# One more third of a token tile by gathered rows: the first 128 tokens instead of 96, with the routing stage's low parts moved from VectorE to GpSimd

## The reference, cut to what matters

```python
s = jnp.einsum("thpc,pkc->thpk", q, sub_keys)          # scores against 2 x 128 half keys, 8 heads
s1, i1 = lax.top_k(s[:, :, 0], 16); s2, i2 = lax.top_k(s[:, :, 1], 16)
top_s, pos = lax.top_k(cand_s, 16)                     # best 16 of the 16 x 16 sums, for each head
gate = jax.nn.softmax(top_s, axis=-1)
...
u = u_tab[ib]                                          # 128 experts for each token, 1024 numbers each
act = jax.nn.gelu(jnp.einsum("td,ted->te", xb, u), approximate=False)
return jnp.einsum("te,ted->td", act * gb, v_tab[ib])
```

## Time and profile before

| | |
|---|---|
| Median of 3 runs | 2227.98 us (2227.13 to 2233.2) |
| Profiled execution: time, span | 2232.91 us, 2231.2 us |
| Mean granted TensorE clock | 0.974 of full speed |
| PE busy | 2069.1 us (93%) |
| DVE, ACT, POOL busy | 1405.5, 829.9, 445.4 us |
| DMA moved | 396.68 MB in 239664 packets, 114912 of them under 512 B |
| The store of a 64-token block of gates | 4096 KB, 28.1 us from issue to landing |
| A load of a U chunk | 512 KB, 4.0 us |

### The profile page before, as it was taken

How to read it: one execution, slowest core, us unless ns; L and a number is a source line. 1 busy time by engine, 2 the same in 40 slices (tenths; PEclk the granted TensorE clock), 3 DMA queues, 4 the chain that set the end, 5 groups by cost and what they waited for, 6 DMA issues and landing times.

```text
span 2231.2 us, 30598 instructions
## 1 busy us (share of the span) xinstructions
PE 2069.1 (93%) x11732; PEld 1844.5 (83%) x11732; DVE 1405.5 (63%) x2647; ACT 829.9 (37%) x1271; POOL 445.4 (20%) x557
## 2 busy tenths in 40 slices
PE   7889888889988799999999998888999999999999
PEld 7766666666656578889999998888999999999999
DVE  5442442532532564399999687777277777777777
ACT  4333433432432443233333465555333333333332
POOL 3132032032031100001000132221022323232322
PEclk9999999999999799999999999999999999999999
DMA  3210200200200642246554599999789999999996
GB/s 117 71 38 1 80 30 11 75 25 10 76 29 10 213 153 76 78 126 184 174 168 146 170 268 271 278 270 268 261 291 325 325 326 319 325 319 323 321 325 234
DMA packets 239664, 396.68 MB, mean 178 GB/s; under 512 B 114912, under 2 KB 164256, under 8 KB 239520
## 3 DMA queue, kind: packets, MB, share of 16 engines
q1 hardware_dynamic: 209568, 287.66, 40.5%
q0 software_dynamic: 29952, 107.07, 14.3%
HBM read 335.85 MB, written 58.72 MB: 177 GB/s over the span
## 4 chain that ended last, share of the span: by engine, by line
PE 54%; DVE 5%; DMA 5%; ACT 1%; issue 1%; SPq 0%; ACTq 0%; DVEq 0%
PE psE L84 17%; PE psE L86 17%; PE psE L85 17%; DMA raw<-in_peer_u 4%; DVE shared L1706 1%; PE psE L1911 1%; ACT expert_hi L1381 1%; PE psE L1912 1%; DVE expert_lo L1538 1%; PE psE L1869 1%; DVE shared L1613 1%; DVE few_gathered L1695 1%; DMA raw<-in_w_mixers 0%; DVE half_index L1617 0%; DVE w_lo L1748 0%
## 5 line engine op out<-in xcount | busy, mean ns | idle before, releaser
L1381 ACT ACTIVATE expert_hi<-raw 128x1024 fp32r<-128x1024 f32 x288 | 305.0, 1059 | 522.1 <-PE psE L86 446.9
L1538 DVE TENSOR_TENSOR expert_lo<-raw,expert_hi 128x1024 fp32r<-128x1024 f32 x288 | 351.8, 1223 | 214.2 <-ACT expert_hi L1381 211.5
L84 PE MATMUL psE<-w_hi,expert_hi 128*128 128x416 f32 x1024 | 360.9, 352 | 15.5 <-DVE w_lo L1748 15.5
L84 PE MATMUL psE<-x2h,expert_hi 128*128 128x416 f32 x1024 | 368.0, 359 | 5.0 <-DVE expert_lo L1538 5.0
L86 PE MATMUL psE<-x2h,expert_lo 128*128 128x416 f32 x1024 | 361.3, 353 | 0.0
L85 PE MATMUL psE<-x2l,expert_hi 128*128 128x416 f32 x1024 | 360.9, 352 | 0.0
L85 PE MATMUL psE<-w_lo,expert_hi 128*128 128x416 f32 x1024 | 358.8, 350 | 0.0
L86 PE MATMUL psE<-w_hi,expert_lo 128*128 128x416 f32 x1024 | 358.7, 350 | 0.0
L84 PEld LDWEIGHTS psE<-w_hi,expert_hi 128*128 128x128 f32 x1024 | 192.2, 188 | 25.7 <-issue 20.9
L84 PEld LDWEIGHTS psE<-x2h,expert_hi 128*128 128x128 f32 x1024 | 194.6, 190 | 8.2 <-DVE expert_lo L1538 6.7
L85 PEld LDWEIGHTS psE<-x2l,expert_hi 128*128 128x128 f32 x1024 | 194.9, 190 | 2.1
(11 more groups left out here) (290 smaller groups left out, 3544.8 us busy)
## 6 DMA issues: line engine op xcount, KB each, us to landing
raw<-in_peer_u SPq DMA_DIRECT2D x128, 512.0 KB, 4.0
raw<-in_peer_v SPq DMA_DIRECT2D x128, 512.0 KB, 6.5
expert_acts<-gelu SPq DMA_DIRECT2D x128, 208.0 KB, 4.9
shared<-expert_acts SPq DMA_DIRECT2D x128, 208.0 KB, 4.2
shared<-expert_gates SPq DMA_DIRECT2D x128, 176.0 KB, 5.5
expert_gates<-shared SPq DMA_DIRECT2D x5, 4096.0 KB, 28.1
ring<-in_w_xonly SPq DMA_DIRECT2D x24, 512.0 KB, 3.4
ring<-in_w_full SPq DMA_DIRECT2D x16, 512.0 KB, 3.9
```

Of the source, the lines that this page charges most:

```text
L84: nc.tensor.matmul(out, sh, mh, start=first, stop=False)
L1381: nc.scalar.activation(wh[:, s % R, :], raw[:, s % R, :], ACT.Copy).then_inc(S["hi_done"], 1)
L1538: v.tensor_tensor(wl[:, s % R, :], raw[:, s % R, :], wh[:, s % R, :].bitcast(F32), ALU.subtract).then_inc(S["lo_done"], 1)
```

## The change

FEW becomes 128 and MANY 384: the first tile of tokens is wholly gathered, one token to a partition, with no spreading, no groups and no `fold`. The steps are 128 dots and 128 additions (before: 96 and 96). 78 dots stand between the routing steps of tiles 1 to 3, 26 to a tile, over `few_ring`; 46 beside the pairs and 4 behind them, over `u_ring`; the additions all in the V stage. The rows of x stay in PSUM (`rows_x`, two banks), and the dots read them there. In the U stage the low parts of chunks 3 to 78 are written by GpSimd, in the same queue as the gathers; VectorE writes those from 79 on. A tile's turn comes at chunks 34, 55 and 76 (ROUTED_AT) and the pairs begin at chunk 76: 48 pairs. The DRAM tensor of the gates is laid out by blocks, so that a block's store is 32 KB in one piece for each partition; the V stage loads gates for 4 chunks at once, in pieces of 1 KB. The loads at the start of `back` are in another order, and two loads on GpSimd wait for the mixers' high parts.

```diff
-GROUPS = ((0, 64), (64, 32))
-FEW = sum(count for _, count in GROUPS)
-FIRST_OPS = 48
+FEW = P
+TILE_DOTS = 26
+ROUTE_DOTS = (NT - 1) * TILE_DOTS
+FIRST_DOTS = P
 MANY = SEQ - FEW
-ROUTE_CHUNKS = 16
-PAIRS_A = NT * ROUTE_CHUNKS
+ROUTED_AT = (13, 34, 55, 76)
+PAIRS_A = ROUTED_AT[-1]
-STORED = MANY - BLOCK
+STORED = (BLOCKS - 1) * BLOCK
+GATE_CHUNKS = 4
+        rows_x = ps[:, ROW_BANK:ROW_BANK + 2, :].rearrange("p b d -> p (b d)")
...
             def store_rows(b):
-                t0, t1 = max(b * BLOCK - SHIFT * GATE_TOKENS, 0), (b + 1) * BLOCK - SHIFT * GATE_TOKENS
-                sp.dma_start(gates_dram[:, :, t0:t1].rearrange("j i t -> i j t"),
-                             rows[b % 2][:, :, BLOCK - (t1 - t0):]).then_inc(rows_stored[b % 2], 16)
+                sp.wait_ge(S["gates_moved"], 2 * PER_BLOCK * (b + 1))
+                sp.dma_start(gates_dram[:, b, :, :], rows[b % 2]).then_inc(rows_stored[b % 2], 16)
...
-                sp.dma_start(gates_in[:, r, :], gates_dram[j]).then_inc(w_loaded[r], 16)
+                if j % GATE_CHUNKS == 0:
+                    slot = j // GATE_CHUNKS % 2
+                    sp.dma_start(gates_in[:, slot, :, :, :], gates_dram[:, :, j:j + GATE_CHUNKS, :]).then_inc(
+                        gates_loaded[slot], 16)
...
         def _(pool):
+            def low(s):
+                pool.wait_ge(S["lo_done"], s)
+                pool.wait_ge(S["hi_done"], s + 1)
+                nc.gpsimd.tensor_tensor(wl[:, s % R, :], raw[:, s % R, :], wh[:, s % R, :].bitcast(F32),
+                                        ALU.subtract).then_inc(S["lo_done"], 1)
+            pool.wait_ge(S["mixed_hi"], DC - 2)
...
+            for j in range(3, ROUTED_AT[0]):
+                low(U + j)
             pool.wait_ge(S["few_picked"], 2)
-            for g, (t0, count) in enumerate(GROUPS):
-                for f in range(P // count):
-                    for out_, in_ in ((which[g], picked_expert), (few_gate[g], picked_gate)):
-                        pool.dma_start(out_[f * count:(f + 1) * count, :],
-                                       in_[t0:t0 + count, f * count:(f + 1) * count]).then_inc(few_spread, 16)
+            for n in range(R):
+                gather(n)
+            sent = R
+            for j in range(ROUTED_AT[0], PAIRS_A + 3):
+                low(U + j)
+                while sent < min(R + (j + 1 - ROUTED_AT[0]) * ROUTE_DOTS // (PAIRS_A - ROUTED_AT[0]), ROUTE_DOTS):
+                    gather(sent)
+                    sent += 1
...
             def turn_rows(k):
-                for (t0, count), b in zip(GROUPS, ROW_BANKS):
-                    for f in range(P // count):
-                        last = nc.tensor.matmul(
-                            ps[f * count:(f + 1) * count, b + k // 4, (k % 4) * P:(k % 4 + 1) * P],
-                            normed[:, k % 2, t0:t0 + count], c["ident"][:, :], start=True, stop=True)
+                nc.tensor.matmul(ps[:, ROW_BANK + k // 4, (k % 4) * P:(k % 4 + 1) * P], normed[:, k % 2, 0:FEW],
+                                 c["ident"][:, :], start=True, stop=True).then_inc(S["rows_turned"], 1)
```

More of the change, by code:

```diff
@@ L1191 @@
 BLOCKS = -(-MANY // BLOCK)
-SHIFT = (BLOCKS * BLOCK - MANY) // GATE_TOKENS
-STORED = MANY - BLOCK
+STORED = (BLOCKS - 1) * BLOCK
+GATE_CHUNKS = 4
 STORES = [len(range(b, BLOCKS - 1, 2)) for b in range(2)]
 HALF_ROWS = KEYS * BLOCK
[L1196 to L1199, removed]
+ROW_BANK = 0
+TURN_BANK = 2
+GELU_AT = 1
 MIX, OUT, QUERY, U, V = 0, DC, 2 * DC, 4 * DC, 4 * DC + KEYS
@@ L1295, in back @@
         gathered = [sem(f"few_gathered{r}") for r in range(R)]
-        few_spread = sem("few_spread")
+        gates_loaded = [sem(f"gates_loaded{r}") for r in range(2)]
         mixed_loaded = [sem(f"mixed_loaded{k}") for k in range(DC)]
@@ L1347, in _ @@
                 sp.dma_start(mixer_out[:, k, :], mixed[k]).then_inc(mixed_loaded[k], 16)
-                if k % 4 == 3:
-                    load(k // 4 + 1)
-            load(3)
+            for r in range(1, R):
+                load(r)
             sp.dma_start(keys[:, :, :], ap["keys"]).then_inc(keys_loaded, 16)
@@ L1594, in take_query @@
                 v.tensor_tensor(query[:, q % 2, :], ps[:, 2 + q % 2, :], rstd[:, :], ALU.mult).then_inc(S["query_ready"], 1)
-            ahead = itertools.chain([None] * 3, range(3, N))
-            def low_next():
-                j = next(ahead)
-                if j is not None:
-                    low(U + j)
+            few = itertools.count()
+            gaps = itertools.count()
+            def dots_next():
[3 more added lines that the diff above has]
+                        few_next()
             count = 0
@@ L1749, in low_w @@
                                 ALU.subtract).then_inc(S["w_lo_done"], 1)
-            done = 0
-            for t0, few in GROUPS:
-                v.tensor_copy(fold[:, t0:t0 + few], c["ident"][:, 0:few]).then_inc(S["folded"], 1)
-                for f in range(1, P // few):
-                    done += 1
-                    dve.wait_ge(S["folded"], done)
-                    v.tensor_tensor(fold[:, t0:t0 + few], fold[:, t0:t0 + few],
-                                    c["ident"][:, f * few:(f + 1) * few], ALU.add).then_inc(S["folded"], 1)
-                done += 1
             low(0)
@@ L1762, in _ @@
                 mixed_row(k)
-                if k == 3:
-                    low(1)
+            low(1)
             for m in range(DC):
@@ L1785, in _ @@
                 route(i)
-            low_next()
             take(NT - 1)
+            dve.wait_ge(S["lo_done"], U + PAIRS_A + 3)
             for p in range(PAIRS_B):
                 one_hot(p)
-                if 2 <= p < 2 + FIRST_OPS:
-                    few_first(p - 2)
-                low_next()
-            for j in ahead:
-                low(U + j)
+                if p >= 2:
+                    few_next()
+                low(U + PAIRS_A + 3 + p)
+            trailing = FIRST_DOTS - ROUTE_DOTS - (PAIRS_B - 2)
+            rest = N - PAIRS_A - 3 - PAIRS_B
+            for k in range(rest):
+                for _ in range(k * trailing // rest, (k + 1) * trailing // rest):
+                    few_next()
+                low(U + N - rest + k)
             low(V)
@@ L1805, in _ @@
                     low(V + j + 3)
[L1806 to L1809 removed]
+                if j == GELU_AT + 2:
+                    few_weigh()
+                for _ in range(few_upto(j - 1) if j else FIRST_DOTS, few_upto(j)):
+                    few_next()
                 if j + 1 < N:
@@ L1950, in _ @@
                 activations(j)
-                if j < PAIRS_A + 1 and j % ROUTE_CHUNKS == 0 and j > 0:
-                    turn(j // ROUTE_CHUNKS - 1)
+                if j in ROUTED_AT[1:]:
+                    turn(ROUTED_AT.index(j))
                 if PAIRS_A <= j < PAIRS_A + PAIRS_B:
```

188 lines of the change are left out of this document (83 added, 105 removed).

## The result

The changed kernel takes 2156.75 us (median of 4 runs, 2155.93 to 2159.93) against 2227.89 before: ratio 0.968, 95% interval 0.966 to 0.970. That is 71 us faster where 120 were forecast, and 2 us above the range. The profiled execution took 2157.28 us with a span of 2155.5, 75.6 under its counterpart before.

What follows compares the result with a forecast made beforehand. TensorE, busy nearly throughout the expert stages, was taken as the bound, a matmul's price going by columns. -83.6 - 3.8 - 5.8 - 26 + 12 - 13 = -120 on 2228.0 gave 2108 us, range 2080 to 2155.

Steps and rivals of the forecast that it cites:

- columns, 6144 matmuls: Expert stages: matmuls go from 416 to 384 columns, a step of 175.2 ns, 13.6 ns less each; -83.6 us.
- start of the U stage: Before U: row turning, six matmuls become one, saves 5.3 us, reordered first loads perhaps 0.5; together -5.8 us.
- loss in the routing: Routing beside U: new losses 7 + 6 + 4 = 17 us, some 5 of old idling gone; +12, bounds -5 and +62.
- loss in V: V stage: of 21 us lost, 8 left, 4 for double turns and 4 for transfers; -13 us.
- Rival C: Expert matmuls: the 0.19 us weight load binds, so fewer columns give nothing; 2192 us, chance 0.03.
- it fits in 4.205, barely: V stage: chain from ScalarE's hi to w_lo's end, 3.96 us plus about 0.1, fits a 4.205 us chunk.
- Rival A: Pairs and V: transfers bind, shorter chunks ask more than DMA gives; up to 2160 us, half 2134, chance 0.20.
- large packets are nearer to V's row: Store at the pairs: of a remaining loss between 0 and 46 us, takes 8; with 34 gone, -26 us.
- Exclusion of VectorE's operations and GpSimd's: Routing tiles: VectorE operations with two SBUF inputs wait for GpSimd lows, 0 to 12 us a tile, 6 taken.
- The stall of 7 us for the low of chunk 13: Routing: GpSimd waits for tile 0's experts, issues four gathers, then the low at 1008.5; TensorE wants it at 1001.3.
- rival B: Routing: GpSimd binds, in-order gathers behind dots and lows of 2.6 us; some 50 us, 2146 us, chance 0.18.
- Rival D: Routing: slower than before, VectorE holds up GpSimd's lows, chunk 6.1 us or more; 2284 us at 7 us, chance 0.03.

Runs made afterwards that it cites:

- e1: Changed kernel, V stage writes the low part of the next chunk's activations ahead of the weights' low part and the addition; 2133.1 us, ratio 0.957.
- e12: e10 with each block's store sent in four quarters, one chunk apart; 2091.0 us, ratio 0.939.
- e5: Changed kernel with the old DRAM layout of the gates, in pieces of 256 bytes; 2189.7 us, ratio 0.982.
- e11: Changed kernel without the gathers beside the pairs (48 of 50 over u_ring left out, dots kept, output differs); 2131.2 us, ratio 0.957.
- e13: e12 with V's first loads (activations of the first four chunks and their gates) two chunks earlier; 2081.5 us, ratio 0.934.
- e2: Changed kernel with rank and index of the candidates in PSUM instead of SBUF; 2141.4 us, ratio 0.960.
- e3: Changed kernel with tile 0's exponents and gathers four chunks later (ROUTED_AT 17 for 13); 2153.7 us, ratio 0.967.
- e8: Changed kernel with the diffs of e2 and e3 together; 2146.0 us, ratio 0.962.
- e10: Changed kernel with the edits of e1, e2 and e9 together; 2106.5 us, ratio 0.945.
- e9: e2 with a tile's 26 dots spread over the 16 gaps by the time VectorE has, not evenly; 2137.3 us, ratio 0.958.

## Why the prediction was wrong

Losses are what a stage takes over its chunks at the step's price and its pairs at 0.96 us. Between the starts of the table lie 65 chunks, 51 chunks with pairs and 12 chunks before, and 77, 47 and 4 after (us of the profiled executions):

| term of the sum | forecast | measured |
|---|---|---|
| columns, 6144 matmuls | -83.6 | -95.2 |
| four pairs fewer | -3.8 | -3.8 (taken) |
| start of the U stage | -5.8 | -14.2 |
| loss in the routing | +12 | +33.0 (12.0 to 45.0) |
| loss at the pairs | -26 | -17.3 (39.1 to 21.8) |
| loss at the turn to V | 0 | +11.0 (0.2 to 11.2) |
| loss in V | -13 | +10.7 (20.3 to 31.0) |

The last four are 21.0 + 8.7 + 11.0 + 23.7 = 64 us worse, the first and the third 11.6 + 8.4 = 20 better; 120 + 20 - 64 = 76 is what the two executions differ by. Two starting points were misread: from the first pair's start to the last one's are 51 steps and not 52, so that 39 us were lost there and not 34, and V took 600.1 us by the earlier trace rows, not 601.

*Columns: right, a little small.* A step of 173.3 ns, under both of my lines, so a matmul of 384 columns saves 15.5 ns and not 13.6. Rival C, the weight load as a floor, is out: the load still reads 0.19 us, and the step fell.

*Start of U: right in kind.* The merge, from its first matmul to its last, is 8.4 us shorter (740.6 to 944.0 before, 734.9 to 929.9 after), in place of 5.8. The other 5.7 arise in the first 735 us, where the change only puts two small tables elsewhere in SBUF. With one and the same code there, that point lies between 732.3 and 741.2 in the profiled executions of after and of the twelve experiments, and the 740.6 of before lies within. Between 160 and 180 us the granted clock was 0.83 before and 1.00 after. So nothing here shows that these 5.7 are the change's.

*V: the step "it fits in 4.205, barely" failed*, and it is the dearest. It compared the chain from the start of `hi` to the end of `w_lo` with a chunk, and left out the ends that close the loop: 0.21 us from the chunk's first matmul to `hi`, and 0.15 from `w_lo` to the next matmul. The trace of before had it: a chunk's first matmul started at 1691.27 and `hi` at 1691.53, so that 0.26 + 3.96 + 0.15 = 4.37 was under the 4.53 of a chunk then, and over 4.205. That with TensorE faster the bound would pass to this chain was among my signs of error, but no rival had it, and I priced it at nothing. e1 shows it: same bytes, same work, other order, 26 us less in V. Timeline of TensorE, before:

```profile
1691.27 0.35 PE L84 MATMUL psE<-w_hi,expert_hi 128*128 128x416 f32 x1
```

*Rival A, transfers bind:* out as I meant it, for e1 and e12 move the same bytes faster, at 334 and 326 GB/s. The 324 of before was what was asked for.

*The store: right on SP, wrong on what stays.* The issue of 20.50 us is gone, and e5 brings it back, at 12 us in the pairs. I worked out the rest as volume against rate and took 8. What stayed was one transfer's landing: a gather of 512 KB beside the 4 MB store lands in some 10 us, over two slots, and the low and the one-hots stand behind it in VectorE's queue. e11 takes the gathers away, e12 the burst, and the stage is 244.9 and 244.8 us, 4 over 47 x 5.12, so that 17.6 of the 21.8 were this wait. The step that failed is "large packets are nearer to V's row". I asked what the dots beside the pairs cost VectorE and DMA, not what they wait for.

*The turn to V: not in the sum.* ScalarE's `w_hi(0)` needs gates loaded after the last store and weighed, 11.3 us late; before, the loss there was nothing (54.6 us for 12 chunks of 4.53). e13 and e11 take off 5.4 and 9.8 of it, from its two ends.

*Routing: right in kind, a third in size.* Exclusion of VectorE's operations and GpSimd's was priced at 2 us a tile, 6 in all, and the part of it that e2 takes away cost 17.4 us, since it stretches the gathers too, and what GpSimd loses shows as TensorE's wait. The stall of 7 us for the low of chunk 13 didn't come: GpSimd waited 3.75 us for tile 0's experts, and TensorE 1.36 us for the low. Another stood there that I didn't name: ScalarE's exponents of tile 0, in the queue ahead of `hi` and gelu, hold TensorE for 8 us, five chunks earlier. Nor may that be added as it stands, for e3 and e8 remove it and the stage gets no shorter. That GpSimd and VectorE wait for each other in turn, so that time won at one tile is lost at the next, is my reading of the waits that grew. Of rival B's 50 us two thirds came: the loss in the stage grew by 33, though GpSimd is busy for only 238 of 280 us in the window and waits for others in the rest. Rival D is out with lows of 2574 ns.

*Open.* 22 us are still lost in the routing of e13 (342.4 against 77 x 4.16 = 320.3). In e10, with the same routing, the wait behind the exponents (7.8), those for lows (5.5) and the first pair's for its one-hot matrices (3.9, as in the kernel before) account for 17. What the lower clock beside that first wait adds is argued from the window of 0.74 and wasn't tried by itself. The exponents were moved only together with tile 0's gathers (e3, e8), and not with the order of dots of e9.

## What to carry to other kernels

When an edit makes the bounding engine faster, take each loop of waits that closes once per tile and add all of it: the releasing instruction, each start behind it, the semaphore, the weight load. One that had under 0.2 us of room (4.37 in 4.53) becomes the bound, and here the cure was to swap two instructions. Moving work to an idle engine must be priced by what stands behind it in each queue, with the landing time of its transfers during the largest burst beside it; and a queue's stall that seems to be one event may be a lockstep that comes back elsewhere.

## What the hardware did that I had not expected

- An indirect gather's issue on GpSimd took 2.82 to 3.06 us beside VectorE's compares with two inputs in SBUF, for 0.94 alone; the mean of the stage's gathers fell from 1124 to 969 ns when one of these inputs lay in PSUM. VectorE's side paid as well: 2890 ns on the mean for 2280.
- The step of matmuls of 384 columns is 173.3 ns, 1.2 to 2.7 ns below the lines through the steps at 264, 416 and 512, and under the 174.5 to 176 that I took as bounds.
- Splitting a 4096 KB store in quarters, one chunk apart, made each 1024 KB quarter land in 9.1 us and took the gathers' wait from 38 us (e10) to 13, and no engine waited for the store; two chunks apart, the last quarter was late for its buffer.
